# A two-layer decoder step: the prompt's gates computed beside the second projection pass, and the normalisation of each first half written out as a pipeline over single tiles

## What is computed

```python
def rmsnorm(x, g):
    r = lax.rsqrt(jnp.mean(xf * xf, axis=-1, keepdims=True) + EPS)
    return xf * r * g
...
h_p, h_s = rmsnorm(y_p, norm_pre[l]), rmsnorm(y_s, norm_pre[l])
z = h @ w_in                       # columns q, k, v, f, xq, gate (layer 0)
lf = jax.nn.log_sigmoid(f + b_f)   # 2048 x 8: an output, too
c = jnp.cumsum(lf, axis=1)
s = q @ k.T * scale + (c_i - c_k)  # causal softmax of s, times v
...
b = concat(mixer(z), memory_attention(z)) * silu(gate)
y = y + rmsnorm(b @ w_out, norm_post[l])
```

## Time and profile before

| | us |
|---|---|
| median of 3 runs | 3914.15 (3910.99 to 3914.58) |
| the profiled execution, its own time | 3909.49 |
| its span, first to last instruction | 3908.0 |
| PE busy | 3497.3 (89%) |
| DVE busy | 1840.8 (47%) |
| ACT busy | 1335.8 (34%) |
| n00, from its first issue to the next block's | 3.47 to 54.92 |
| gates' block, to the attention's first load | 1698.87 to 1728.05 |
| n10, from its first issue to the next block's | 2743.23 to 2793.42 |

### The profile page before, as it was taken

How to read it: one execution, slowest core, us unless ns; L and a number is a source line. 1 busy time by engine, 2 the same in 40 slices (tenths; PEclk the granted TensorE clock), 3 DMA queues, 4 the chain that set the end, 5 groups by cost and what they waited for, 6 DMA issues and landing times. The chain is left out here.

```text
span 3908.0 us, 54215 instructions
## 1 busy us (share of the span) xinstructions
PE 3497.3 (89%) x19825; PEld 3044.4 (78%) x19825; DVE 1840.8 (47%) x3346; ACT 1335.8 (34%) x2541; POOL 459.4 (12%) x678
## 2 busy tenths in 40 slices
PE   5999898899999999968888887999499899995999
PEld 5999898788888887747777775788499878774787
DVE  3332223366666654537777766433322245565432
ACT  3112322245545543435555553111212244310111
POOL 1320000001100110113322231000000001121000
PEclk9999999999999999979999998899799999997999
DMA  3444333567767764432222222332333343566332
GB/s 121 122 126 146 110 105 99 152 210 235 236 225 239 241 193 136 132 103 76 74 74 82 74 60 92 108 113 81 103 107 111 114 125 114 172 191 187 101 113 77
DMA packets 409291, 515.57 MB, mean 132 GB/s; under 512 B 50743, under 2 KB 298040, under 8 KB 407503
## 3 DMA queue, kind: packets, MB, share of 16 engines
q1 hardware_dynamic: 378055, 415.12, 34.5%
q0 software_dynamic: 27552, 84.82, 6.5%
q10 hardware_dynamic: 3456, 12.58, 1.0%
HBM read 388.57 MB, written 124.22 MB: 131 GB/s over the span
## 5 line engine op out<-in xcount | busy, mean ns | idle before, releaser
L459 ACT ACTIVATE z_st_p<-bank 128x352 f32<-128x352 f32 (+3 forms) x325 | 168.0, 519 | 740.4 <-PE bank L434 739.8
L1599 PE MATMUL bank<-w_hi_o,b_hi_o 128*128 128x512 f32 x816 | 328.7, 403 | 63.1 <-DVE w_lo_o L1641 63.1
L434 PE MATMUL bank<-h00hi,w_hi_p 128*128 128x352 f32 x984 | 322.9, 328 | 17.6 <-DVE w_lo_p L401 7.5
L1600 PE MATMUL bank<-w_hi_o,b_lo_o 128*128 128x512 f32 x816 | 324.5, 398 | 0.0
L1601 PE MATMUL bank<-w_lo_o,b_hi_o 128*128 128x512 f32 x816 | 324.4, 398 | 0.0
L434 PE MATMUL bank<-h00hi,w_lo_p 128*128 128x352 f32 x984 | 317.5, 323 | 0.0
L434 PE MATMUL bank<-h00lo,w_hi_p 128*128 128x352 f32 x984 | 317.3, 322 | 0.0
L399 DVE CAST w_hi_p<-w_raw_p 128x1024 fp32r<-128x1024 f32 (+1 forms) x130 | 89.3, 687 | 446.9 <-PE bank L434 388.4
L434 PE MATMUL bank<-h01hi,w_hi_p 128*128 128x512 f32 x656 | 271.1, 413 | 12.6 <-DVE w_lo_p L401 11.6
L852 DVE TENSOR_TENSOR pT_lo_fa<-bank,pT_hi_fa 128x512 fp32r<-128x512 f32 (+2 forms) x320 | 194.0, 607 | 139.7 <-ACT pT_hi_fa L794 139.0
L434 PE MATMUL bank<-h01lo,w_hi_p 128*128 128x512 f32 x656 | 258.5, 394 | 0.0
(11 more groups left out here) (353 smaller groups left out, 8790.9 us busy)
## 6 DMA issues: line engine op xcount, KB each, us to landing
k_raw_sf<-in_cache_fox_k SPq DMA_DIRECT2D x128, 512.0 KB, 4.1
v_raw_sf<-in_cache_fox_v POOLq DMA_DIRECT2D x128, 512.0 KB, 4.3
z<-z_st_p SPq DMA_DIRECT2D x112, 512.0 KB, 3.0
w_raw_p<-in_fox_w_in SPq DMA_DIRECT2D x80, 512.0 KB, 5.1
b_raw_o<-bT SPq DMA_DIRECT2D x32, 768.0 KB, 7.4
w_raw_p<-in_pool_w_in SPq DMA_DIRECT2D x48, 512.0 KB, 4.9
out<-tok_p SPq DMA_DIRECT2D x64, 256.0 KB, 2.6
w_raw_o<-in_w_out ACTq DMA_DIRECT2D x24, 512.0 KB, 3.7
```

The costliest lines, as they stand in the source:

```text
L434: last = nc.tensor.matmul(bank[:, 0:width], wt[:, u, k, :], h[:, k, at0:at0 + width], start=(m == 0), stop=(m == MM - 1))
L459: nc.scalar.activation(z_st[0:rows_t, t % 2, at0:at0 + width], bank[0:rows_t, 0:width], tiles[t][2]).then_inc(z_read, 1)
L1599: nc.tensor.matmul(out, bh, w_hi[:, k, cols], start=(k == 0), stop=False)
L1600: nc.tensor.matmul(out, bl, w_hi[:, k, cols], start=False, stop=False)
```

## The change

**Normalisation.** The loop over pairs is gone; the nine tiles are written out one by one. Rows have three buffers instead of two, and the load of the gain comes behind the first load of rows. The squares go to a buffer `sq` of their own, so they wait for their rows only. The transposes use all eight banks in turn (four tiles of two banks), so they wait for the subtractions of four tiles earlier. Sum, mean, root and inverse have one column per tile, one small operation each per tile.

**Gates.** The block becomes a stream of 16 steps beside p01, plan (33, 0) to (40, 16), thus between tiles 33 and 40, behind the memory attention in each slot. One PSUM bank (bank 7) replaces five: the four groups of matmuls take it in turn, each waiting for the copy of the group before, and the copies overwrite `mag`. The operations, their sizes and the three transfers are the same.

The core of the diff:

```diff
@@ norm_transpose
+    XR, TR = 3, 4
...
+            for t, (src, n, _) in enumerate(tiles):
+                if t >= XR:
+                    sp.wait_ge(xn_d, t - XR + 1)
+                sp.dma_start(x[0:n, t % XR, :], src).then_inc(x_in[t % XR], 16)
+                if t == 0:
+                    sp.dma_start(g_bc[:, :], gain.partition_broadcast(P)).then_inc(g_in, 16)
...
+            square(0)
+            for t in range(NT + 1):
+                if t < NT:
+                    n = tiles[t][1]
+                    act.wait_ge(ms_d, t + 1)
+                    nc.scalar.activation(ms[0:n, t:t + 1], ms[0:n, t:t + 1], ACT.Sqrt).then_inc(rt_d, 1)
+                if t + 1 < NT:
+                    square(t + 1)
+                for j in range(2 if t else 0):
+                    act.wait_ge(tr_d, 2 * (t - 1) + j + 1)
+                    nc.scalar.copy(hT_hi[split_to(t - 1, j)], bank(t - 1, j)).then_inc(hi_d, 1)
...
+                for j in range(2 if t > 1 else 0):
+                    dve.wait_ge(hi_d, 2 * (t - 2) + j + 1)
...
+            for t, (_, n, _) in enumerate(tiles):
+                pe.wait_ge(xn_d, t + 1)
+                if t >= TR:
+                    pe.wait_ge(lo_d, 2 * (t - TR) + 2)
@@ prompt_gates
-        @block.scalar
+    BANK, Z = banks[5], NQ // 2
...
+    STEPS = 16
...
+            if i == 6:
+                sp.wait_ge(lf_d, 1)
+                sp.dma_start(lf_prompt.rearrange("n p h -> p n h"), lf[:, :, :]).then_inc(out_d, 16)
+            if i == STEPS - 1:
+                sp.wait_ge(row_d, 4)
+                sp.dma_start(cT[:, :], mag[:, :]).then_inc(out_d, 16)
+                sp.wait_ge(out_d, 32)
...
+            if 11 <= i < 15:
+                g = i - 11
+                if g == 0:
+                    pe.wait_ge(scan_d, 5)
+                    pe.wait_ge(tri, 2)
+                else:
+                    pe.wait_ge(row_d, g)
@@ decoder_step
+                        late = prompt_gates(nc, sems, room, const, banks[2:8], z0, F_ROW, fox_b_f, fox_lf_p, cT, [(33, 0), (40, 16)],
+                                            rows.when(XQ), ends_f)
...
-        prompt_gates(nc, const, banks, z0, F_ROW, fox_b_f, fox_lf_p, cT)
```

More of the change, by code:

```diff
@@ L87, in make_constants, with norm_transpose @@
     return dict(ident=ident, ones=ones, ones_r=ones_r, ident_b=ident_b, mask_b=mask_b)
-def norm_transpose(nc, tag, const, banks, looped, single, gain, hT_hi, hT_lo):
-    n_pairs = looped.shape[0] // P // 2 if looped is not None else 0
+def norm_transpose(nc, tag, const, banks, rows, sample, gain, hT_hi, hT_lo):
     ident = const["ident"]
+    XR, TR = 3, 4
+    tiles = [(rows[t * P:(t + 1) * P, :], P, t * P) for t in range(rows.shape[0] // P)] + [(sample, NS, rows.shape[0])]
+    NT = len(tiles)
     with ExitStack() as s:
@@ L99, in norm_transpose @@
         g_bc = c.sb("g_bc", [P, D])
[L100 to L111, removed]
@@ L112, in norm_transpose @@
-        hi_done = c.sem("hi_done")
-        lo_done = c.sem("lo_done")
-        block = s.enter_context(nc.Block())
[L116 to L127, removed]
+        x, xn = c.sb("x", [P, XR, D]), c.sb("xn", [P, 2, D])
@@ L129, in _, with split_to @@
+        def split_to(t, j):
+            return slice(None), slice(4 * j, 4 * j + 4), slice(tiles[t][2], tiles[t][2] + tiles[t][1])
         @block.sync
         def _(sp):
[L131 to L136, removed]
@@ L145, in body @@
[L145 to L159, removed]
@@ new lines, in act @@
+    def act(act):
+        for i in range(STEPS):
+            if i == 1:
+                act.wait_ge(f_in, 32)
+                nc.scalar.activation(mag[:, :], fT[:, :], ACT.Abs, bias=b_col[:, :]).then_inc(log_d, 1)
+            if i == 2:
+                act.wait_ge(log_d, 1)
+                nc.scalar.activation(mag[:, :], mag[:, :], ACT.Exp, scale=-1.0).then_inc(log_d, 1)
+            if i == 3:
+                act.wait_ge(log_d, 2)
+                nc.scalar.activation(mag[:, :], mag[:, :], ACT.Ln, bias=1.0).then_inc(log_d, 1)
+            if 11 <= i < 15:
+                n = i - 11
+                act.wait_ge(ct_d, n + 1)
+                nc.scalar.copy(mag[:, n * 512:(n + 1) * 512], BANK[0:FH, :]).then_inc(row_d, 1)
+            yield
@@ new lines, in pe @@
+    def pe(pe):
+        for i in range(STEPS):
+            if i == 5:
+                pe.wait_ge(sub_d, 1)
+                for n in range(NQ):
+                    last = nc.tensor.transpose(BANK[:, n * FH:(n + 1) * FH], low[:, n * P:(n + 1) * P], ident[0:FH, 0:FH])
+                last.then_inc(tr_d, 1)
+            if 11 <= i < 15:
+                g = i - 11
[4 more added lines that the diff above has]
+                    pe.wait_ge(row_d, g)
+                for n in range(4 * g, 4 * g + 4):
+                    out = BANK[0:FH, n % 4 * P:(n % 4 + 1) * P]
+                    nc.tensor.matmul(out, lf[:, n, :], upto[:, :], start=True, stop=False)
+                    last = nc.tensor.matmul(out, pad[0][:, Z - 1 + n, :], ones[:, :], start=False, stop=True)
+                last.then_inc(ct_d, 1)
+            yield
@@ L555, in fox_attention @@
+    return Work(STEPS, plan, dict(sp=sp, pool=pool, pe=pe, act=act, dve=dve))
 def fox_attention(nc, const, banks, zT, cT, bT, v_out):
```

202 lines of the change are left out of this document (89 added, 113 removed).

## The result

The changed kernel takes 3855.35 us (median of 4 runs, 3847.93 to 3860.56) against 3912.57 us (3908.91 to 3914.58, 4 runs) for the kernel before: a ratio of 0.9853, 95% interval 0.9835 to 0.9872, 57 us less. Run once more on another occasion it took 3857.06 us, ratio 0.9855 (0.9837 to 0.9874). The profiled execution took 3847.93 us; it happens to be the fastest of its four, so its span is 61.6 us shorter, more than the medians are apart.

What follows compares the result with a forecast made beforehand. PE, busy 3497 of 3908 us, was taken as the bound, leaving 411 idle us to win. Terms -29.2 + 9.4 - 0.6 - 32.0 = -52.4, counted from 3912, gave 3860 us, range 3849 to 3877.

Steps and rivals of the forecast that it cites:

- The gates' block, -29.2: Between the pass's last store and the attention's first load: the block goes and the attention's loads start there, -29.2 us.
- The work in p01, +9.4: Gates' work beside the memory attention: 7.9 us on PE paid nearly in full, plus 1.5 for stalls; between +5 and +20.
- The stalls behind long operations: In p01, long gate operations on ACT and DVE delay the memory attention's chain: +1.5 us, bounds nothing to some 12.
- The table at the attention's start, -0.6: The attention's first exponential finds its table already loaded: -0.6 us, bounds 0 and -1.3.
- The normalisations, -32.0: n00 and n10: DVE sets the pace, 3.05 us a tile in place of 4.85; -16.3 and -15.7 us.
- the sign that asked for no such wait over 0.5: In n00 of the changed kernel's profile, no wait of the squares for rows should exceed 0.5 us.
- The chain in p01: Rival: gates' ACT and DVE operations hit the memory attention in full, p01 grows 20 to 30 us; 3875, chance 0.1.
- the 14 that would have refuted it: In p01, the prediction is wrong if PE's waits for exponentials grow from 8.2 to over 14 us.
- wait for a tile of weights: In p01, the prediction is wrong if SP holds weights back behind a wait for the gates; nothing was counted for this.
- The ring: Rival in the normalisations: three loads in flight land later than 4.2 us, 4.1 us per tile; 3874, chance 0.08.
- The block did leave the path: Answers a rival: moving the gates' block does nothing, as the attention could not start earlier; 3889, chance 0.03.
- The attention's low clock: Rival: PE's low clock at the attention's start lasts on, at 150 us more of it 3928 us; chance 0.02.

Runs made afterwards that it cites:

- e2: The kernel before with only the gates' stream moved beside p01, the normalisations still loops over pairs: 3893.15 us, ratio 0.9950.
- e6: The changed kernel with each pair of gate matmuls issued twice, 32 more matmuls: 3863.0 us in one run.
- e7: The changed kernel with a second activation over 8x2048 behind each of the gates' three long ones on ACT: 3861.41 us in one run.
- e8: The kernel before with one tiny exponential at the end of ACT's part of the gates' block, loading the exponential's table ahead: 3909.12 us in one run.
- e10: The kernel before, still in pairs, with squares in their own buffer and the scaling waiting for the transposes of the pair before: 3901.82 us in one run.
- e1: The kernel before with the change's normalisation alone, the gates keeping their block: 3876.9 us, ratio 0.9907.
- e11: The changed kernel with the gates' logarithm replaced by an absolute value of the same size, removing two table loads: 3854.4 us in one run.
- e3: The changed kernel with two buffers of rows instead of three: 3870.08 us in one run.
- e12: The changed kernel run once more with no edit: 3857.06 us, ratio 0.9855.
- e5: The changed kernel with squares written into the buffer that the transposes read, as before: 3862.22 us in one run.

## Why the prediction was right, point by point

- **The gates' block, -29.2.** Measured from the last eviction to the first load: -28.9, and -28.5 in e2. Right.
- **The work in p01, +9.4.** Measured +10.6. Of it the matmuls took 8.0 where 7.0 were counted, and e6 shows 7.0 for 32 more of them, so 1 us belongs to the four groups. The trace places it: each group makes the pass's next matmul come 2.0 us later, 1.75 us by its own starts and 0.25 us at its edges, and PE has no wait there, so it is not the copies. Why the edges cost this was not tested. The transposes took 1.3, not 0.95. The stalls behind long operations were 1.3 against 1.5. That bound ran from 0 to 12 us, and the reason given for the low end (other matmuls cover most of 1.9 us) holds only in part: the three activations cost 0.8, 0.0 and 0.5 us each, and by e7 little of the slack is left behind the first of them. That the sum came so near is in part luck. The step "PE's work is paid, the others' nearly not" held.
- **The table at the attention's start, -0.6.** Worth 1.1 us by e8, 0.7 to 0.8 by the same distance in e10 and e1, and not to be told from the scatter of transfers in the total. By the Trainium skill, ScalarE: Activation LUTs, section "What ACT_TABLE_LOAD costs", each switch would be 2.66 us; the load's row shows 1.28 us with the next activation straight behind, and e11 shows 0.5 us for two.
- **The normalisations, -32.0.** Measured -20.7 and -19.3, **-40.0**: the mechanism was right (the engines no longer take turns, DVE sets the pace), four sizes were off, three of them in one direction. In n00 the first scaling was done at 11.1 instead of 12.4, since the rows landed 3.4 us after their issue when nothing stood ahead of them. The second scaling came 2.6 us behind the first, not 1.9, as its square waited 1.0 us for rows, against the sign that asked for no such wait over 0.5; this was the one size off the other way. The pace was 2.65 instead of 3.05 us: I had added whole durations and 0.2 us of handshakes, but the starts of DVE's rows are closer than their durations (scaling to next operation 1.20, two subtractions 1.20, the small ones 0.06 and 0.19; sum 2.65), and the root is taken on ACT while DVE subtracts. The end took 2.0 instead of 2.9 us.
- **The rivals.** The chain in p01 did not give way (10.6 us, not 25; PE's waits 9.3 us, below the 14 that would have refuted it), and no wait for a tile of weights shows there. The ring was not the bound (3.5 us landing, 2.65 a tile); with one buffer less it is (e3). The block did leave the path. The attention's low clock did not last longer: the granted clock was 0.50 from 1691.7 to 1715.5, for 24 us, and from 1726.8 to 1750.6 before, also 24 us; from the first exponential to the first issue of n10 passed 996.1 us, 996.5 before.
- **The sum.** The stretches give -28.9 + 10.6 - 40.0 = -58.3 and 1.1 for the table; the medians say -57 and -54, the prediction -52. It fell short by the 8 us of the normalisations and lost 1.2 us of that in p01. Between the stretches the profile shows further shifts, 3.5 us more up to the late part of p01 and 4.4 us less behind n10; the second goes with PE's clock: from the first weights of p10 to the end, the granted clock was 0.50 for 110 us in the change's trace, 121 before and 133 in e12, the same kernel as the change, and that stretch took 1110.2, 1114.6 and 1119.4 us. The first differs by up to 7 us between kernels that do the same there. Neither is put down to a step of the change. So the total was missed by 5 us, less than the normalisations alone were: the misses and this scatter partly cancelled, which is luck.

## What to carry to other kernels

A block in which the engines take turns was shortened here by the third buffer and by the order together, not by removing the wait with a large number: of 5.03 us a pair that squares waited for transposes, removing the wait alone gave 0.6 us a pair, as the next load stood right behind it. Cost the pace of a full engine by the distances of its starts, not by durations plus handshakes. Work moved beside a stage that one engine fills costs that engine's share of it in full, and the other engines' share only beyond the slack of the chain that feeds it; double the suspect operation to see how much slack is left, and look at the granted clock of the stretch before the whole difference is put down to it.

## What the runs showed of the hardware

Four rows of DVE (scaling, small operation, two subtractions in one row, small operation) that last 1.28, 0.15, 1.28 and 0.15 us repeat every 2.65 us, less than the sum of 2.86: the end of one row lies behind the start of the next by up to 0.1 us. A tile's rows of 512 KB landed in 3.4 us with no load ahead of them, in 3.5 on median in n00 of the changed kernel, where the later ones go out 2.65 us apart, and, where two go out 1.2 us apart (e10), the second in 4.3 to 4.7. Beside the memory attention, from the 17th eviction to the last, PE's granted clock fell to 0.50 for 3.4 us in four of the fourteen traces (e1, e2, e5, e7), each time behind waits of PE, and that cost 1.4 to 1.6 us; in e6 it stayed at 1.00 behind a wait as long. The start of the attention varied by 2.2 us between two traces of one kernel (16.7 us in the change, 18.9 in e12).
